# Head pairs on halves of the TensorE array in attention, and four indexer heads on its four row groups

## What is computed

```python
def dsa_block(q, qi, wi, q_pos, k, v, ki, k_pos, top_k):          # top_k = 256
    idx_dot = einsum('bthi,bsi->bths', qi, ki)                    # indexer: 8 heads of 32 numbers
    score = einsum('bth,bths->bts', wi, relu(idx_dot))            # one score per query and key
    score = where(k_chunk <= q_chunk, score, NEG_INF)
    _, sel = top_k(score, 256)                                    # the kernel makes a mask of it
    logits = einsum('bthd,btjd->bthj', q, k[sel]) * HEAD_DIM ** -0.5   # 8 heads of 64, one shared key and value
    probs = softmax(where(valid, logits, NEG_INF))
    return einsum('bthj,btjd->bthd', probs, v[sel])
```

## Time and profile before

| | us |
|---|---|
| median of three runs | 1910.65 |
| the profiled execution | 1912.12 |
| its span | 1910.4 |
| TensorE busy (share of the span) | 1616.1 (85%) |
| VectorE busy | 853.6 (45%) |
| ScalarE busy | 359.4 (19%) |
| GpSimd busy | 247.4 (13%) |
| mean granted TensorE clock | 0.897 of full |

### The profile page before, as it was taken

The page is one execution under the profiler, slowest core; times in us unless marked ns, Lnnn a source line. Parts: engine busy times, 40 slices in busy tenths (PEclk is TensorE's granted clock), DMA queues, the critical chain, the costliest instruction groups (busy, mean ns, idle before and its releaser), DMA issues. The chain is left out here.

```text
span 1910.4 us, 17684 instructions
## 1 busy us (share of the span) xinstructions
PE 1616.1 (85%) x6056; PEld 948.0 (50%) x6056; DVE 853.6 (45%) x1730; ACT 359.4 (19%) x734; POOL 247.4 (13%) x333
## 2 busy tenths in 40 slices
PE   7799968779788899999979999799993097999960
PEld 1455623368644566666647777564552043444430
DVE  1311229755067999999972334341113011111118
ACT  2311110010145011111114455201110010111112
POOL 0000020000031011111100000001221411222214
PEclk9899989867589899999989999799996598999985
DMA  9100036420010312221001200242221679999987
GB/s 340 57 4 4 6 106 203 115 20 3 2 31 12 113 57 64 81 82 57 24 29 43 93 1 1 115 139 77 90 94 45 123 294 337 365 370 366 370 312 254
DMA packets 167818, 233.91 MB, mean 122 GB/s; under 512 B 31909, under 2 KB 131877, under 8 KB 167413
## 3 DMA queue, kind: packets, MB, share of 16 engines
q1 hardware_dynamic: 156226, 202.34, 32.8%
q0 software_dynamic: 9376, 28.53, 3.8%
q10 hardware_dynamic: 2148, 2.13, 0.3%
HBM read 191.65 MB, written 39.19 MB: 121 GB/s over the span
## 5 line engine op out<-in xcount | busy, mean ns | idle before, releaser
L1153 DVE TENSOR_SCALAR_CACHE_REDUCE tk_hits<-sc,tk_cand 128x384 bf16<-128x384 f32 (+6 forms) x217 | 250.4, 1154 | 7.7
L1119 PE MATMUL ps<-hT,gt_w 128*128 128x352 f32 (+1 forms) x768 | 240.1, 471 | 12.7 <-DMA gt_w<-in_w_glu 12.7
L1903 PE MATMUL ps<-ex_wgu,ex_xT 128*128 128x512 f32 x416 | 188.1, 606 | 13.7 <-DMA ex_wgu<-in_w_up 12.6
L1119 PEld LDWEIGHTS ps<-hT,gt_w 128*128 128x128 f32 x768 | 146.8, 191 | 102.3 <-DMA gt_w<-in_w_glu 13.3
L1500 PE MATMUL ps<-hT,mergedT 128*128 128x512 f32 (+1 forms) x288 | 127.2, 601 | 4.7 <-DMA op_wr<-in_w_route_expert 4.7
L1903 PEld LDWEIGHTS ps<-ex_wgu,ex_xT 128*128 128x128 f32 x416 | 78.9, 195 | 104.7 <-issue 104.7
L1119 PE MATMUL ps<-zT,gt_w 128*128 128x352 f32 (+1 forms) x384 | 120.9, 468 | 0.0
L1331 DVE CUSTOM_DVE_ANT_0 at_s<-ps,mask 128x1024 f32<-128x1024 f32 (+8 forms) x76 | 58.8, 777 | 103.9 <-PE ps L1243 91.4
L1976 DVE TENSOR_TENSOR ex_hid<-ex_silu,ps 128x256 f32<-128x256 f32 x26 | 10.9, 421 | 191.1 <-ACT ex_silu L1946 191.1
L1119 PEld LDWEIGHTS ps<-zT,gt_w 128*128 128x128 f32 x384 | 73.0, 190 | 44.0
L1922 PE MATMUL ps<-ex_wd,ex_hidT 128*128 128x512 f32 x208 | 93.7, 593 | 1.0 <-DVE ex_hidT L1982 1.0
(11 more groups left out here) (422 smaller groups left out, 2160.3 us busy)
## 6 DMA issues: line engine op xcount, KB each, us to landing
ex_wgu<-in_w_gate SPq DMA_DIRECT2D x28, 1024.0 KB, 6.8
ex_wgu<-in_w_up SPq DMA_DIRECT2D x28, 1024.0 KB, 9.5
ex_wd<-in_w_down SPq DMA_DIRECT2D x27, 1024.0 KB, 9.6
sp_ada_w<-in_w_ada SPq DMA_DIRECT2D x14, 1024.0 KB
gt_w<-in_w_in SPq DMA_DIRECT2D x16, 512.0 KB, 5.2
cb_y<-y_dram SPq DMA_DIRECT2D x16, 512.0 KB, 5.3
merge_left_dram<-qiT SPq DMA_DIRECT2D x8, 544.0 KB, 6.3
mg_gb<-gate_b_dram SPq DMA_DIRECT2D x8, 544.0 KB, 3.8
```

The source lines that it names most:

```text
L1119: i = nc.tensor.matmul(m.ps[:, seq % 8, 0:n], w[:, c % NB, at + k, :], rhs[:, k, lo:lo + n], start=k == 0, stop=k == nk - 1)
L1153: return v.tensor_scalar(hits[0:r, 0:w], m.sc[0:r, c:c + w], scalar, 0.0, ALU.is_ge, ALU.add, accum_out=cnt[0:r, j:j + 1])
L1903: j = nc.tensor.matmul(m.ps[:, 2 + b, :], xT[:, b, k, :], wgu[:, b, k, :, :].rearrange("p a n -> p (a n)"), start=k == 0, stop=k == KD - 1)
```

## The change

In the **indexer** a step is now four heads. Head h of a group of four has its 32 rows at partitions 32h to 32h+31 of `qiT` and of `kiT`, so the four matmuls of a 512-key piece use the four row groups of the array and write four different PSUM banks; there are two slots of four banks. One relu reads four banks; `ix_relu` has two buffers of four heads. VectorE's operations stay the same in number and size. GpSimd's memsets and copies of `ix_q` go. In **attention** a unit of a prompt tile is one pair of heads (tiles 4 to 7), two pairs (2 and 3) or four (0 and 1). The pair's scores alternate between rows 0:64 and 64:128 of the array, into banks 0 and 1 or 2 and 3. In `values` v is now the stationary (128x64), on columns 0:64 for the even head and 64:128 for the odd one, and the transposed probabilities move; the output comes out transposed, so the output's own transposes and the sample's DMA go. In their place the reciprocals of the sums are spread and transposed (`reciprocals`, `widen`, `widths`). Scores run one unit ahead instead of two.

```diff
@@ index_scores
-    units = [(i, t, k, w) for i, t in enumerate(tiles) for k, w in pieces(PAST + DEC if t == PT else P * (t + 1))]
-    steps = [(i, t, k, w, h) for i, t, k, w in units for h in range(IH // 2 if t == PT else IH)]
+    steps = [(t, k, w, a) for t in tiles for k, w in pieces(PAST + DEC if t == PT else P * (t + 1))
+             for a in range(1 if t == PT else 2)]
+    halves = [pieces(w, 512) for _, _, w, _ in steps]
+    h_at = [sum(map(len, halves[:n])) for n in range(len(steps) + 1)]
...
-        relu = sb("ix_relu", [P, 4, 1024])
-        qz = sb("ix_q", [P, 2, IH, P])
+        relu = sb("ix_relu", [P, 2, 4, 1024])
...
-                            j = nc.gpsimd.tensor_copy(qz[rows, i % 2, x:IH:4, :], m.qiT[rows, :, t * P:(t + 1) * P])
...
+                    for c, (k, x) in enumerate(halves[n]):
+                        s = h_at[n] + c
+                        if s >= 2:
+                            pe.wait_ge(rl, s - 1)
+                        for h in range(4):
+                            rows = slice(ID * h, ID * (h + 1))
+                            if t == PT:
+                                q, keys = qs[rows, :, :].rearrange("p a n -> p (a n)"), m.kiTs[rows, k0 + k:k0 + k + x]
+                            else:
+                                q, keys = m.qiT[rows, a, t * P:(t + 1) * P], m.kiT[rows, k0 + k:k0 + k + x]
+                            i = nc.tensor.matmul(m.ps[:, 4 * (s % 2) + h, 0:x], q, keys, start=True, stop=True)
+                        i.then_inc(ps, 1)
...
+                    if n >= 2:
+                        act.wait_ge(acc, 4 * (n - 1))
+                    for c, (k, x) in enumerate(halves[n]):
+                        s = h_at[n] + c
+                        act.wait_ge(ps, s + 1)
+                        nc.scalar.activation(relu[:, n % 2, :, k:k + x], m.ps[:, 4 * (s % 2):4 * (s % 2) + 4, 0:x],
+                                             ACT.Relu).then_inc(rl, 1)
...
+                    dve.wait_ge(rl, h_at[n + 1])
+                    for h in range(4):
...
@@ attention
+    def pairs_of(t):
+        n = 1 if t > 3 else 2 if t > 1 else 4
+        return [tuple(range(j, j + n)) for j in range(0, H // 2, n)]
+
+    units = [(p, t, js) for p, t in enumerate(order) for js in pairs_of(t)]
...
+                    pe.wait_ge(sd, d_at[u])
+                    for jj, j in enumerate(js):
+                        at = jj * (1024 // len(js))
+                        for k, w in pieces(width[u], 512):
+                            for x in range(2):
+                                half = slice(HD * x, HD * (x + 1))
+                                i = nc.tensor.matmul(slot[x][:, at + k:at + k + w], m.attnT[half, j, t * P:(t + 1) * P],
+                                                     m.kT[half, k:k + w], start=True, stop=True)
                         i.then_inc(sp_, 1)
...
+                def reciprocals(p):
+                    n = r_at[p]
+                    pe.wait_ge(rw, p + 2)
+                    pe.wait_ge(te, n - 1)
...
-                        i = nc.tensor.matmul(m.ps[:, 6, h * HD:(h + 1) * HD], pT[0:x, u % 2, b, :], src[0:x, b, :],
-                                             start=b == 0, stop=b == len(blocks[u]) - 1)
+                    for b, (k, w) in enumerate(pieces(width[u], P)):
+                        for x in range(2):
+                            half = slice(HD * x, HD * (x + 1))
+                            if t == PT:
+                                out = m.ps[half, 6 + p % 2, js[0] * DEC:(js[0] + 1) * DEC]
+                                i = nc.tensor.matmul(out, m.vs[0:w, b, :], pT[0:w, u % 2, b, DEC * x:DEC * (x + 1)],
+                                                     start=k == 0, stop=k + w == width[u])
+                            else:
+                                out = m.ps[half, 6 + p % 2, js[0] * P:(js[-1] + 1) * P]
+                                src = pT[:, u % 2, x * nb_ + b:x * nb_ + b + 2 * nb_ * (np_ - 1) + 1:2 * nb_, :]
+                                i = nc.tensor.matmul(out, m.v[:, b, :], src, start=k == 0, stop=k + w == width[u])
...
                 scores(0)
-                scores(1)
                 for u in range(NU + 1):
-                    if u + 2 < NU:
-                        scores(u + 2)
+                    if u + 1 < NU:
+                        scores(u + 1)
                     if u < NU:
                         transposes(u)
+                    if closes[u] is not None:
+                        reciprocals(closes[u])
                     if u:
                         values(u - 1)
...
+                exps(0)
+                for u in range(NU):
+                    copies(u)
+                    if closes[u] is not None:
+                        widths(closes[u])
+                    if u + 1 < NU:
+                        exps(u + 1)
...
-                    sp.dma_start(dst[:, :, x, :], os_[DEC * x:DEC * (x + 1), :, :]).then_inc(osm, 16)
```

More of the change, by code:

```diff
@@ L928, in index_scores @@
             "loaded", "repeated", "transposed", "evacuated", "z_loaded", "z_transposed", "z_copied", "new_keys"))
-        before = [next(n for n, s in enumerate(steps) if s[0] == i) for i in range(len(tiles))]
         with nc.Block() as block:
@@ L942, in _ @@
                     sp.dma_start(ws[DEC * x:DEC * (x + 1), :], m.wi[0:DEC, PT, IH // 2 * x:IH // 2 * (x + 1)]).then_inc(wsl, 16)
-                sp.wait_ge(acc, before[at + 1])
+                sp.wait_ge(acc, 4 * (sample[-1] + 1))
                 sp.dma_start(other[:, :], m.sc[DEC:P, SC_SAMPLE:SC_SAMPLE + PAST + DEC]).then_inc(ol, 16)
@@ L986, in cached_keys @@
                     i.then_inc(zp, 1)
-                for n, (i, t, k0, w, h) in enumerate(steps):
-                    if n == before[at]:
-                        pe.wait_ge(rl, n)
+                for n, (t, k0, w, a) in enumerate(steps):
+                    if n == sample[0]:
+                        pe.wait_ge(rl, h_at[n])
                         cached_keys()
@@ L1019, in _ @@
                 nc.vector.tensor_copy(m.kiTs[:, PAST:], m.kiT[:, SEQ:NT]).then_inc(kd, 1)
-                for n, (_, t, k0, w, h) in enumerate(steps):
-                    if n == before[at]:
+                for n, (t, k0, w, a) in enumerate(steps):
+                    if n == sample[0]:
                         for g in range(2 * CB // 4):
@@ L1201, in attention @@
 def attention(nc, m, A):
-    order = range(PT, -1, -1)
-    units = [(p, t, h) for p, t in enumerate(order) for h in range(H // 2 if t == PT else H)]
-    first = [units.index((p, t, 0)) for p, t in enumerate(order)]
-    NU = len(units)
-    chunks = [pieces(keys_of(t)[0]) for _, t, _ in units]
-    blocks = [pieces(keys_of(t)[0], P) for _, t, _ in units]
-    groups = [[b[i:i + 4] for i in range(0, len(b), 4)] for b in blocks]
-    c_at = [sum(map(len, chunks[:u])) for u in range(NU + 1)]
-    g_at = [sum(map(len, groups[:u])) for u in range(NU + 1)]
+    order = list(range(PT, -1, -1))
+    def pairs_of(t):
+        n = 1 if t > 3 else 2 if t > 1 else 4
+        return [tuple(range(j, j + n)) for j in range(0, H // 2, n)]
+    units = [(p, t, js) for p, t in enumerate(order) for js in pairs_of(t)]
+    NU = len(units)
+    first = [next(u for u, x in enumerate(units) if x[0] == p) for p in range(TILES)]
+    sample = lambda u: units[u][1] == PT
+    width = [keys_of(t)[0] for _, t, _ in units]
+    heads = [1 if t == PT else 2 * len(js) for _, t, js in units]
+    blocks = [pieces(heads[u] * width[u], P) for u in range(NU)]
+    groups = [[b[i:i + 4] for i in range(0, len(b), 4)] for b in blocks]
+    chunks = [pieces(width[u]) if sample(u) else [] for u in range(NU)]
+    drains = [len(chunks[u]) or heads[u] for u in range(NU)]
+    made = [len(chunks[u]) or len(units[u][2]) for u in range(NU)]
+    c_at, d_at, e_at = ([sum(x[:u]) for u in range(NU + 1)] for x in (made, drains, heads))
+    closes = [units[u][0] - 1 if u in first and u else None for u in range(NU)] + [TILES - 1]
+    g_at, r_at, n = [], {}, 0
+    for u in range(NU + 1):
+        g_at.append(n)
+        n += len(groups[u]) if u < NU else 0
+        if closes[u] is not None:
+            r_at[closes[u]] = n
+            n += 1
     SCALE = HD ** -0.5
@@ L1294, in _ @@
-                output(PT)
             @block.vector
@@ new lines, in widen @@
+                def widen(p):
+                    a, b = e_at[first[p]], e_at[first[p + 1] if p + 1 < TILES else NU]
+                    dve.wait_ge(er, b)
+                    v.reciprocal(rs[:, a:b], sm[:, a:b]).then_inc(rr, 1)
+                    dve.wait_ge(rr, p + 1)
+                    if p:
+                        dve.wait_ge(tp, r_at[p - 1] + 1)
+                        v.tensor_copy(rb[:, :, :].rearrange("p j (x d) -> p (j x) d", x=2), bc(rs[:, a:b], 2, HD)).then_inc(rw, 1)
+                    else:
+                        for x in range(2):
+                            half = slice(HD * x, HD * (x + 1))
```

(13 more changed lines are left out.)

239 lines of the change are left out of this document (104 added, 135 removed).

## The result

The changed kernel takes 1833.81 us (median; 1826.54 to 1836.97) against 1911.31 (1907.11 to 1912.71), a ratio of 0.959 with a 95% interval of 0.9562 to 0.9618. I forecast 1857, within 1838 to 1896.

A forecast was written before the change was run, and what follows sets the result against it. It took TensorE to bound both the indexer and attention. 1912.12 - 12 (indexer) - 45 (prompt tiles) + 1.2 (sample) = 1856.3, 1855 as a median, plus 2 for thin covers: 1857 us, range 1838 to 1896.

The forecast's parts named there:

- The indexer: Indexer block: VectorE becomes the bound instead of TensorE, with 79 us from start to end; -12 us.
- two large waits: VectorE in the indexer: 5.5 us idle at the start and 5.7 us behind the cached keys.
- half-step: Indexer, 4 heads x 512 keys on TensorE: at most 1.7 us at half clock with four row groups side by side.
- the sample: Sample part of attention: 68 value records at 0.054 us, shape changes and longer preparation; +1.2 us.
- My 133.6: Prompt tiles of attention: tiles 7 to 0 plus reciprocals take 133.6 us against 178.6, so -45 us.
- skew in the scores: Attention, scores of a tile 7 pair: one record of skew may stay, so 1.9 us instead of 1.72.
- shape changes: Attention, a pair of tile 7: three changes of array shape instead of one, 0.2 us each, 0.6 in all.
- the 2 us of reserve: Whole kernel: 2 us added to the forecast because each thin cover can only cost.
- B: Attention and indexer: row halves and groups run in turn with a stationary of 128 columns; 1894 us, chance 0.08.
- C: Attention: ScalarE's loop decides in all tiles, through slower copies or longer links; 1873 us, chance 0.11.
- D: Attention: no overlap pays at all, so the kernel gets slower; 1932 us, chance 0.03.
- E: Attention's prompt tiles: TensorE's clock drops to 1.2 GHz, so the kernel gets slower; 1940 us, chance 0.04.

The follow-up runs named there:

- e8: Changed kernel, but the sample's values move 128 columns a record instead of 64, loads unchanged; 1837.08 us, ratio 0.9647.
- e3: Changed kernel, but values issues all records of the even head's column half before all of the odd head's; 1858.35 us, ratio 0.9728.
- e13: Changed kernel with one unused 512-column ScalarE copy between the two exponentials of each pair of tiles 7 to 4; 1832.07 us, ratio 0.9599.
- e10: Changed kernel, but scores of tiles 7 to 4 issue one head before the other, each matmul four times (16 records against 16); 1976.85 us, ratio 1.0329.

## Why the prediction was right, and where it failed

**The indexer** came out as worked: -12.6 for -12. VectorE's busy time of 64.2 us and its two large waits, which answer to the earlier trace rows, are near the forecast (5.5 and 5.7):

```profile
530.70 0.75 DVE L1023 TENSOR_SCALAR sc<-ix_relu,wi 128x1024 f32<-128x1024 f32 x1 [5.39 <-ACT ix_relu L1003]
...
571.00 0.75 DVE L1023 TENSOR_SCALAR sc<-ix_relu,ix_w_sample 128x1024 f32<-128x1024 f32 x1 [5.18 <-ACT ix_relu L1003]
```

The row groups overlap fully. At clock 0.50 four weight loads come together every 0.86 us, which is one record of 512 columns at that clock:

```profile
587.59 0.35 PEld L989 LDWEIGHTS ps<-kiT,qiT 32*128 32x128 f32 x4 [0.50 <-issue]
588.45 0.35 PEld L989 LDWEIGHTS ps<-kiT,qiT 32*128 32x128 f32 x4 [0.50 <-issue]
```

A half-step is therefore 1.72 us. The 3.07x that the Trainium skill gives for four row tiles (TensorE: Matmul & The Clock Gate, "Measured speedup vs the span model") would have made it 2.2 by my estimate; the measurement decides, and it has 4x here.

**Attention** took the rest of the miss: 234 us became 170 where I had 190, in three steps.

One, 8.0 us, is a slip in the sum and no mechanism. The 178.6 us that I took as "before" for the prompt tiles began at 1043.40, with the transposes of tile 7's second head. The scores of tile 7's first four heads and the transposes of the first lie ahead of that, as this timeline of the kernel before shows for the third and fourth scores, and so they were in the 55.4 us that I left to the sample:

```profile
1035.08 1.93 PE L1243 MATMUL ps<-kT,attnT 64*128 64x512 f32 x4
1036.94 1.09 PE L1256 MATMUL ps<-ident,at_s 128*128 128x128 f32 x8
...
1042.02 1.45 PE L1243 MATMUL ps<-kT,attnT 64*128 64x512 f32 x3
1043.40 1.09 PE L1256 MATMUL ps<-ident,at_s 128*128 128x128 f32 x8
```

My 133.6 covered all heads, so this work, four scores of 1.86 us and transposes of 0.9, some 8.3 in all, stood in the forecast twice. It is less by 0.3, as attention ended at 1221.7 and not 1222. Put on the same footing, with scores moved to their tile and the sample's last values to the sample, the prompt tiles went from 186.6 us to 128.9 and the sample from 47.1 to 40.8.

The second is **the sample**: -6.3 for +1.2, a miss of 7.5. I took 0.054 us a record for "64 columns", from L539, whose records move 128, and added 0.4 for shapes: 4.1 us a unit. The unit takes 2.3. Four times 1.8 is 7.2 of the 7.5. e8 shows it from the other side: with 128 columns moved the 68 records take 4.08. e3 gives the pace of one half by itself, 0.068, and the changed kernel half of it, as the halves alternate.

The third is **the sum for the prompt tiles**, 128.9 for 133.6, a miss of 4.7: no skew in the scores (1.73 for 1.9), shape changes of 0.53 in all for 0.6, so a cycle of 6.28 for 6.5 in tile 7. Most of the rest lies in the tiles with units of four and eight heads: cut at their first transposes, tiles 3 and 2 take 22.9 for 25.5 with 0.75 for each tile's reciprocals, tiles 1, 0 and the tail 15.2 for 17.5, the tail at full clock where I had half. ScalarE's loop stayed under TensorE's cycle, as e13 shows for tiles 7 to 4.

**The rest**: 2.7 us in blocks that I held unchanged, within what runs of the same code differ by, and the 2 us of reserve, which nothing used. In sum 0.6 + 8.0 + 7.5 + 4.7 + 2.7 + 2 = 25.5 us, but for rounding the whole miss of 25.6 (1858.3 forecast for the profiled run with the reserve, 1832.7 measured). All the sized terms erred the same way, so my range, closed 19 us under the forecast, was too narrow on that side.

**The rivals.** B (row halves or groups in turn) is out: the 8 records of scores take 1.92 us, not 3.4, and e10 shows what in turn looks like. C is out by the cycle of 6.28 and by e13. D would need values over 0.116 a record; they take 0.054. E is out: the clock is 0.98 over the block and 1.00 at its end. The Trainium skill's warning that tiling does not speed the emptying of PSUM (TensorEngine Tiling (Array Packing), "PSUM Bottleneck") agrees in part with the 10.5 us of waits for copies, 1.7 before. But the transposes themselves are not tiled; what changed for them is that a pair sends 16 in a row through two banks, which one head's 8 just filled. A third bank took nearly all of the wait away (0.6 left) without any faster copy: the ring's depth was the limit, not the copy's rate.

## What to carry to other kernels

Before a difference of two windows goes into a sum, let both begin at the same instruction of the program. Price a record from a row with the same moved and the same loaded columns; a row that matches in one only is a bound for that one. When matmuls use parts of the array, issue the parts in turn, at most four records at a time (six already cost here), and then look again at the ring behind them: an interruption of a burst costs its wait and the latency of starting anew.
